# First block's attention beside the projections: heads in pairs at every second unit instead of one head at every unit

## The reference, cut to what matters

```
def hybrid_mixer(x, w_in, sinks, conv_w, ...):
    proj = einsum('bsd,de->bse', x, w_in)
    y_a = sliding_window_attention(a_q, a_k, a_v, sinks, slopes_a)   # 8 heads of 64, window 128, 2 kv heads
    y_b = gated_short_conv(b_h, b_b, b_c, conv_w)                    # 512 channels, 3 taps
    y_c = moba_attention(c_q, c_k, c_v, slopes_c)                    # 8 heads of 64; one block of 256: causal
    merged = sigmoid(g_a)*(y_a @ w_br_a) + sigmoid(g_b)*(y_b @ w_br_b) + sigmoid(g_c)*(y_c @ w_br_c)
    return merged @ w_out
```

## Time and profile before

| | |
|---|---|
| median of 3 runs | 2946.47 us (2938.63 to 2955.54) |
| the profiled execution, device time | 2949.44 us |
| its span from first to last instruction | 2947.5 us |
| mean granted TensorE clock | 0.989 of full speed |
| PE busy | 2877.5 us, 98% |
| DVE busy | 2045.8 us, 69% |
| ACT busy | 1371.1 us, 47% |
| DMA, mean | 165 GB/s |

### The profile page before, as it was taken

The page is one execution under the profiler, slowest core; times in us unless marked ns, Lnnn a source line. Parts: engine busy times, 40 slices in busy tenths (PEclk is TensorE's granted clock), DMA queues, the critical chain, the costliest instruction groups (busy, mean ns, idle before and its releaser), DMA issues.

```text
span 2947.5 us, 59531 instructions
## 1 busy us (share of the span) xinstructions
PE 2877.5 (98%) x23648; PEld 2776.3 (94%) x23648; DVE 2045.8 (69%) x3307; ACT 1371.1 (47%) x2212; POOL 157.0 (5%) x238
## 2 busy tenths in 40 slices
PE   8999999999999999999999999999999999889998
PEld 8889999889999999999789999999999999779998
DVE  4658786658778777777764476867768667777665
ACT  5555445556546532354544364222642235546544
POOL 0001000001000000010000010000100001000000
PEclk9999999999999999999999999999999999999999
DMA  6436674435666665552212355545646445225564
GB/s 237 151 113 204 227 246 165 147 111 183 224 213 203 205 209 199 171 192 85 76 47 83 100 201 171 207 152 178 213 167 210 144 145 192 75 74 185 178 191 145
DMA packets 148054, 487.55 MB, mean 165 GB/s; under 512 B 16400, under 2 KB 25872, under 8 KB 147728
## 3 DMA queue, kind: packets, MB, share of 16 engines
q1 hardware_dynamic: 126688, 407.22, 41.9%
q0 software_dynamic: 21168, 77.60, 7.7%
HBM read 482.66 MB, written 1.05 MB: 164 GB/s over the span
## 4 chain that ended last, share of the span: by engine, by line
PE 90%; DVE 5%; ACT 2%; issue 1%; DMA 1%; POOL 0%; SPq 0%; DVEq 0%; ACTq 0%; POOLq 0%
PE bank L2161 25%; PE bank L2162 25%; PE bank L2163 25%; PE bank L2079 2%; PE bank L2080 2%; PE bank L2081 2%; DVE wlo L1233 1%; PE aux L2391 1%; PE bank L2409 1%; DVE acc L1848 1%; ACT whi L660 1%; PE aux L2503 1%; PE bank L2239 1%; DMA raw<-in_w_stream 1%; PE aux L2398 0%
## 5 line engine op out<-in xcount | busy, mean ns | idle before, releaser
L2161 PE MATMUL bank<-uhi,whi 128*128 128x256 f32 x4808 | 1350.2, 281 | 5.6 <-ACT vc L875 3.5
L2163 PE MATMUL bank<-uhi,wlo 128*128 128x256 f32 x4808 | 1334.0, 277 | 0.0
L2162 PE MATMUL bank<-ulo,whi 128*128 128x256 f32 x4808 | 1334.0, 277 | 0.0
L1233 DVE TENSOR_TENSOR wlo<-raw,whi 128x1024 fp32r<-128x1024 f32 (+3 forms) x850 | 952.8, 1123 | 331.0 <-ACT whi L660 325.0
L660 ACT CAST whi<-raw 128x1024 fp32r<-128x1024 f32 (+3 forms) x850 | 812.7, 962 | 305.9 <-PE bank L2163 208.6
L2161 PEld LDWEIGHTS bank<-uhi,whi 128*128 128x128 f32 x4808 | 906.5, 189 | 23.9 <-issue 18.2
L2162 PEld LDWEIGHTS bank<-ulo,whi 128*128 128x128 f32 x4808 | 903.3, 188 | 3.9 <-issue 3.6
L2163 PEld LDWEIGHTS bank<-uhi,wlo 128*128 128x128 f32 x4808 | 904.4, 188 | 0.0
L2161 PE MATMUL bank<-yhi,whi 128*128 128x256 f32 x1820 | 517.0, 284 | 4.4 <-DVE ylo L1275 2.4
L2162 PE MATMUL bank<-ylo,whi 128*128 128x256 f32 x1844 | 513.3, 278 | 0.0
L2163 PE MATMUL bank<-yhi,wlo 128*128 128x256 f32 x1820 | 506.5, 278 | 0.0
(11 more groups left out here) (315 smaller groups left out, 3021.7 us busy)
## 6 DMA issues: line engine op xcount, KB each, us to landing
raw<-in_w_stream SPq DMA_DIRECT2D x674, 512.0 KB, 3.6
big<-in_w_ada POOLq DMA_DIRECT2D x64, 512.0 KB, 3.8
vt<-in_w_ada POOLq DMA_DIRECT2D x51, 512.0 KB, 3.7
raw<-in_w_stream SPq DMA_DIRECT2D x80, 256.0 KB, 2.7
raw<-in_w_stream SPq DMA_DIRECT2D x48, 384.0 KB, 3.1
bbb<-in_w_ada POOLq DMA_DIRECT2D x29, 512.0 KB, 5.0
raw<-in_w_stream SPq DMA_DIRECT2D x32, 192.0 KB, 2.4
raw<-in_w_stream SPq DMA_DIRECT2D x16, 128.0 KB, 2.0
```

The costliest lines, as they stand in the source:

```text
L1233: ve.tensor_tensor(wlo[:, u % SLOTS, 0:n], raw[:, u % SLOTS, 0:n], whi[:, u % SLOTS, 0:n].bitcast(F32), ALU.subtract).then_inc(s_low, 1)
L2161: te.matmul(out_, whi[:, u % SLOTS, w], hi(k)[:, cols], start=k == 0, stop=False)
L2162: te.matmul(out_, whi[:, u % SLOTS, w], lo(k)[:, cols], start=False, stop=False)
L2163: ins = te.matmul(out_, wlo[:, u % SLOTS, w], hi(k)[:, cols], start=False, stop=k == plan.kt[u] - 1)
```

## The change

Heads 0 and 1, and heads 2 and 3, of a group are now handled together, at every second unit. `pairs_in_group(i, first)` gives both heads k-1 and k at the unit where k is odd, and nothing at the others. Scores come in pairs at GROUP_AT[g] + 1 and + 3, transpositions at + 11 and + 13, outputs at + 13 and + 15 (before: up to + 14). PE's order within one `attend1` turns round: outputs first, then transpositions, then scores. The groups now begin at 0, 6, 14 and 20, so that all of PE's attention falls on odd units. DVE takes the scores in pairs, ACT copies the turned probabilities in pairs; exponentials and scaling stay one head per unit. The rounding and the remainder of outputs are one unit later relative to the group, and ACT's rounding of the convolution is at unit 28 in place of 27.

```
-GROUP_AT = [0, 7, 14, 21]
+GROUP_AT = [0, 6, 14, 20]
 CONV_AT = {12: 0, 13: 1, 19: 2, 20: 3, 26: 4, 28: 5}
-CONV_HIGH_AT = 27
+CONV_HIGH_AT = 28
...
+        def pairs_in_group(i, first):
+            return [(g, k - d) for g, k in in_group(i, first) if k % 2 for d in (1, 0)]
...
             # ACT
-                for g, k in in_group(i, 10):
+                for g, k in pairs_in_group(i, 10):
                     turned1(k)
-                for first, half in ((13, 0), (15, 1)):
+                for first, half in ((14, 0), (16, 1)):
                     for g, _ in in_group(i, first, 1):
                         high1(g, half)
...
             # DVE
-                for g, k in in_group(i, 0):
+                for g, k in pairs_in_group(i, 0):
                     logits1(l, g, k)
...
-                for first, half in ((13, 0), (15, 1)):
+                for first, half in ((14, 0), (16, 1)):
                     for g, _ in in_group(i, first, 1):
                         low1(g, half)
...
             # PE
             def attend1(l, i):
-                for g, k in in_group(i, 0):
+                for g, k in pairs_in_group(i, 12):
+                    outputs1(g, k)
+                for g, k in pairs_in_group(i, 10):
+                    turn1(g, k)
+                for g, k in pairs_in_group(i, 0):
                     scores1(l, g, k)
-                for g, k in in_group(i, 10):
-                    turn1(g, k)
-                for g, k in in_group(i, 11):
-                    outputs1(g, k)
```

## The result

| | before | after |
|---|---|---|
| median | 2950.53 us (4 runs) | 2918.60 us (4 runs, 2910.08 to 2921.70) |
| ratio | | 0.9896, 95% interval 0.9874 to 0.9918 |
| the profiled execution, device time | 2949.44 us | 2921.70 us |
| its span | 2947.5 us | 2919.9 us |

The changed kernel was timed a second time later, in six runs: 2921.94 against 2944.06, ratio 0.9928, interval 0.9906 to 0.9951. So it is faster, by 1.0% in the first timing and by 0.7% in the second. (The forecast started from 2946.47, the median of three runs before; with a fourth run the median is 2950.53.)

What follows compares the result with a forecast made beforehand. The prediction took PE's own pace as the bound: 2 layers x (6.1 us for fewer visits + 0.6 for pace) = 13.4 us less, from a median of 2946.47 to 2933.1. Predicted 2933, range 2924 to 2944.

Steps and rivals of the forecast that it cites:

- what bounds: In the attention stage only PE's own pace counts; PE is busy for 136.6 of 138.5 us.
- what the loss is: On PE, time lost at each change of the array's shape: 0.40 us for scores alone, 0.34 for outputs alone.
- the counts of 31 and 17 visits: Units per layer with attention on PE: 31 of 36 before, 17 odd units after; prices sum to 37.5 and 31.4 us.
- the cover named for DVE, ACT and the convolution: Slack keeping other engines from delaying PE: 1.5 us for DVE's scaling; losing the convolution's cover costs up to 1 us a layer.
- 6.1 a layer for fewer visits: Gain in PE's attention gaps from handling heads in pairs: 37.5 less 31.4 us a layer.
- the pace: Units behind attention: 7 of 8 slow ones (2.59 us, most take 2.50) become fast, gaining 0.6 us a layer.
- the second head's price: In a pair of scores or outputs on PE, the second head pays its passes alone, 0.65 us.
- The overlap: Rival: second head's first passes run beside the first's last on different array parts; 3.4 us more gained, 2929.7; chance 0.32.
- Changing the part: Rival: moving between array parts costs PE like changing shape, 0.14 us for 12 pairs; 3.4 us back, 2936.5; chance 0.12.
- DVE's lateness: Rival: PE waits for DVE's scaling at +11, 20 us in all, 6.4 more than before, 2953; chance 0.04.
- It doesn't do what it says: Rival: loss is each head's own waits, so fewer visits save nothing; order alone gives 0 to 1 us; chance 0.04.

Runs made afterwards that it cites:

- e6: Kernel before, with scores contracting over all 128 rows and outputs using all 128 weight columns; 2918.34 us in one run against 2948.55.
- e1: Changed kernel with both heads of a pair on the same part of the array; median 2933.42 us in 6 runs, ratio to before 0.9961.
- e4: Kernel before with only PE's order turned to outputs, transposition, scores, one head each; 2948.96 us in one run against 2948.55.
- e5: Changed kernel with a heads ordered 0, 4, 1, 5, 2, 6, 3, 7, so pairs read different rows; median 2917.68 us, ratio to before 0.9895.
- e7: Changed kernel with a transposition between the two outputs at four units a layer; 2934.21 us in one run.
- e9: Changed kernel unchanged, timed again beside another kernel on one chip; median 2921.94 us in 6 runs, ratio to before 0.9928.

## Why the prediction was wrong, point by point

**Right: what bounds, and what the loss is.** PE's own stream is the bound, and the price of attention on it can be read as a gap. The loss is paid at each change of shape (e6), the counts of 31 and 17 visits are what the traces show, and no other engine was late: PE's two waits in the stage are the old ones, so the cover named for DVE, ACT and the convolution held. Taken by itself this part of the forecast was sound: 6.1 a layer for fewer visits, before the pace, where e1's gaps gave 6.0. A pair on the same rows costs what was worked out, 1.71 for 1.70.

**The step that failed: the second head's price.** "I take its passes alone, 0.65, since only the first pass of a shape is held up". This holds only for two heads on the same part of the array, 4 of the 16 pairs of S and O in a layer. The other 12 overlap whole: the second head costs 0.01 to 0.02. The missed term is 8 x 0.63 + 4 x 0.64 = 7.6 us a layer, 15 in all; e1, in which it is taken away, has 7.6 a layer more in its gaps and 7.2 in its stage. The evidence for the choice was a second call within one head, which uses the same part; it says nothing of a second head on the other part, and no row of before did.

**Wrong: the price of the right rival.** The overlap was named and had a third of the chance, but at "at most 0.11 for a pair of O, 0.21 for a pair of S", 3.4 us in all. The unspoken step was that the second head, standing behind all four passes of the first in the program, could start only beside the last one. The trace shows it 13 ns behind the first pass. The lower bound of an unseen cost has to be worked out without such an assumption: in the forecast's own terms, the second head for nothing in 12 pairs leaves 31.4 - 12 x 0.65 = 23.6 us a layer, a gain of 13.9 in place of 6.1, and the range would have reached down to about 2917.5. The gaps measured 23.9.

**Fallen: the other rivals.** Changing the part costs nothing that is seen (OO 1.24, not 2.0). DVE's lateness: PE shows no wait for scaling. "It doesn't do what it says": e4 shows the order alone at 1.9 us, half of it pace.

**Wrong in sign, small: the pace.** 7 of 8 slow units were to go, for a gain of 0.6 a layer. There are 14 afterwards, and by the records the 36 units took 0.4 us longer: 13.6 of gaps less 0.4 is the stage's 13.2. The reading that an exit through O sets the slow pace was wrong; here the unit behind an OO is fast, and those behind the four OOTT, which leave through T, are slow.

**Not to be read too finely: the program's time.** The stages gained 26.4 us in both layers. The medians of the two timings gained 31.9 and 22.1, to either side of it, as runs of one kernel differ by as much.

## What to carry to other kernels

Matmuls that use half of the array's rows or columns should be put in pairs on different halves, directly behind each other: in this kernel the second was then almost free, in plain float32 too, and for the outputs although both heads write the same bank. Small matmuls of another shape than the main stream's should be gathered in as few visits as possible, since each visit here lost 0.33 to 0.39 us for the change alone, while full-size transpositions lost next to nothing. Which heads are neighbours is a choice of layout: permuting heads and their weights' rows made the last four pairs of a layer overlap as well (e5).

## What the runs showed that was not expected

**Full overlap in float32**, as above, of four passes with four. The Trainium skill's section "Key Properties" on the same page says that different tiles load and multiply in parallel; the trace agrees, with a lag of 13 to 14 ns. Program order held back neither head here, only a matmul of another shape between them did (e7).

**Two paces of one and the same product.** Six steps of the same kind of products at 300 us, in layer 0's feed-forward stage, first in the changed kernel, then in the kernel before, with a granted clock of 1.00 in both:

```profile
299.77 0.28 PE L2165 MATMUL bank<-uhi,wlo 128*128 128x256 f32 x1
...
300.45 0.28 PE L2165 MATMUL bank<-uhi,wlo 128*128 128x256 f32 x1
```

```profile
299.78 0.28 PE L2162 MATMUL bank<-ulo,whi 128*128 128x256 f32 x1
...
300.48 0.28 PE L2162 MATMUL bank<-ulo,whi 128*128 128x256 f32 x1
```

0.68 against 0.70; by the records a step takes 0.1133 or 0.1178 us. A pace is kept over units and whole stretches (at times over 300 us) until something breaks the stream; the next stretch may run at either. Within the two stages it is no chance: both layers of the changed kernel, in both of its profiles (the first and e9), have the same 14 slow units. Outside them it differs even between profiles of one kernel: 5,267 and 5,838 slow steps.

Over the twelve profiles, between about 2,200 and 6,850 of some 19,700 such steps outside the stages ran slowly, which costs 10 to 31 us at 4.5 ns each. The time from PE's first to its last matmul, less the stages, went from 2646 to 2663 us; less this cost too, it went from 2628 to 2636. So, by this sum, the pace accounts for about half of the 17 us by which executions differ outside the stages. No run sets the pace on purpose, and what sets it was not found.
